# Second block's attention: where eight gate products stand beside the transposed probabilities and the values

## The reference

```python
q, k, v, x_lru, g_lru, gate_attn, gate_lru = split(u @ w_in)
attn = softmax(causal(rope(q) @ rope(k).T * dh ** -0.5)) @ v     # 8 heads of 128, one block of 256 keys
y_attn = attn @ w_branch_attn
xc = causal_depthwise_conv(x_lru)
r, i = sigmoid(block_diag(xc, w_a)), sigmoid(block_diag(xc, w_i))
a = exp(-8 * r * softplus(-lam)); bx = sqrt(1 - a * a) * (i * xc)
h[t] = a[t] * h[t - 1] + bx[t]
y_lru = (h * gelu(g_lru)) @ w_branch_lru
merged = sigmoid(gate_attn) * y_attn + sigmoid(gate_lru) * y_lru
```

## Time and profile before

| what | value |
|---|---|
| median of 3 runs | 1237.03 us (1235.73 to 1237.9) |
| profiled execution, its own time | 1240.2 us |
| its span, first to last instruction | 1238.4 us |
| TensorE busy | 1074.8 us, 87% |
| VectorE, GpSimd, ScalarE busy | 795.8, 735.4, 466.7 us |
| mean granted TensorE clock | 0.982 |

### The profile page before, as it was taken

How to read it: one execution, slowest core, us unless ns; L and a number is a source line. 1 busy time by engine, 2 the same in 40 slices (tenths; PEclk the granted TensorE clock), 3 DMA queues, 4 the chain that set the end, 5 groups by cost and what they waited for, 6 DMA issues and landing times.

```text
span 1238.4 us, 14907 instructions
## 1 busy us (share of the span) xinstructions
PE 1074.8 (87%) x5042; PEld 735.7 (59%) x5042; DVE 795.8 (64%) x1547; ACT 466.7 (38%) x1013; POOL 735.4 (59%) x445
## 2 busy tenths in 40 slices
PE   6898988999877877787777778899999999999998
PEld 5776544454422322232333223899988997988996
DVE  3367988869668577686675556405354553977977
ACT  5664332231221211211212114545666436434443
POOL 6543766666434444254344332786697985978885
PEclk9999999999999999899999999999999999999999
DMA  7627999999999999999999997763454554555552
GB/s 232 248 85 306 357 420 420 420 419 422 420 422 421 422 421 401 401 405 420 423 421 422 419 420 318 255 186 122 137 166 140 188 172 151 187 173 190 184 190 97
DMA packets 66099, 372.27 MB, mean 301 GB/s; under 512 B 7625, under 2 KB 8753, under 8 KB 32945
## 3 DMA queue, kind: packets, MB, share of 16 engines
q0 software_dynamic: 36864, 268.45, 52.5%
q1 hardware_dynamic: 27696, 98.07, 23.9%
q10 hardware_dynamic: 1472, 4.88, 1.2%
HBM read 369.79 MB, written 1.06 MB: 299 GB/s over the span
## 4 chain that ended last, share of the span: by engine, by line
PE 41%; DMA 30%; DVE 15%; ACT 6%; issue 5%; POOL 3%; DVEq 0%; SPq 0%; POOLq 0%; ACTq 0%
DMA arena<-in_peer_uv,idx_all 28%; PE ps L1796 10%; PE ps L1493 9%; PE ps L1494 9%; PE ps L1495 9%; DVE arena L1275 5%; POOL w_hl L423 2%; DVE yT L1463 2%; DVE arena L1461 2%; DMA ring<-in_weights 2%; PE ps L1842 1%; ACT prob L699 1%; DVE wts L1284 1%; POOL arena L433 1%; ACT w_hl L511 1%
## 5 line engine op out<-in xcount | busy, mean ns | idle before, releaser
L1796 PE MATMUL ps<-arena,prob 128*128 128x512 f32 x1024 | 482.4, 618 | 123.1 <-ACT prob L699 122.2
L433 POOL DMA_INDIRECT arena<-in_peer_uv,idx_all x256 | 288.3, 1126 | 357.9 <-PE ps L1796 324.9
L423 POOL TENSOR_TENSOR w_hl<-ring,w_hl 128x1024 fp32r<-128x1024 f32 x161 | 405.2, 2527 | 119.9 <-ACT w_hl L511 118.4
L1796 PEld LDWEIGHTS ps<-arena,prob 128*128 128x128 f32 x1024 | 189.6, 194 | 404.5 <-ACT prob L699 207.2
L1275 DVE CUSTOM_DVE_ANT_0 arena<-arena,xn 128x1024 f32<-128x1024 f32 x256 | 322.5, 1261 | 154.2 <-DMA arena<-in_peer_uv,idx_all 151.5
L1493 PE MATMUL ps<-xT,w_hl 128*128 128x256 f32 x760 | 218.8, 288 | 5.7 <-DVE arena L1353 2.9
L1494 PE MATMUL ps<-xT,w_hl 128*128 128x256 f32 x760 | 216.0, 284 | 0.0
L1495 PE MATMUL ps<-xT,w_hl 128*128 128x256 f32 x760 | 215.9, 284 | 0.0
L511 ACT ACTIVATE w_hl<-ring 128x1024 fp32r<-128x1024 f32 x161 | 169.3, 1057 | 100.5 <-PE ps L1495 92.6
L692 ACT ACTIVATE gel<-acts 128x2 f32<-128x2 f32 (+1 forms) x130 | 26.4, 203 | 401.6 <-DVE acts L1275 401.6
L1493 PEld LDWEIGHTS ps<-xT,w_hl 128*128 128x128 f32 x760 | 146.9, 193 | 7.8 <-issue 4.5
(11 more groups left out here) (301 smaller groups left out, 1214.7 us busy)
## 6 DMA issues: line engine op xcount, KB each, us to landing
ring<-in_weights SPq DMA_DIRECT2D x178, 512.0 KB, 3.5
arena<-in_peer_uv,idx_all POOLq DMA_INDIRECT x256, 13.5
arena<-in_rg_weights ACTq DMA_DIRECT2D x1, 2048.0 KB, 8.2
x<-in_x SPq DMA_DIRECT2D x2, 512.0 KB, 5.1
bias<-rel_scratch SPq DMA_DIRECT2D x1, 1024.0 KB, 7.9
arena<-in_subkeys SPq DMA_DIRECT2D x1, 1024.0 KB, 5.8
out_x<-x ACTq DMA_DIRECT2D x4, 256.0 KB, 2.1
arena<-in_band SPq DMA_DIRECT2D x1, 768.0 KB, 9.4
```

The lines of the kernel that those rows point to most:

```text
L423: pool.tensor_tensor(pair[:, 1], raw(n), pair[:, 0].bitcast(F32), ALU.subtract).then_inc(w_lo, 1)
L433: pool.indirect_dma_start(uv_slot(n), None, A["peer_uv"], bass.IndirectOffsetOnAxis(idx_all[:, h, c:c + 1], 0))\
L1796: j = pe.matmul(banks(2 + 2 * t + half), diag[:, n % GRING, :], uv_slot(n)[:, D + half * 512:D + (half + 1) * 512], start=False, stop=(h = ...
```

## The change

TensorE issues gate products 8, 9 and 10 each behind two of the six groups of transposes, so the values come after product 10; five gate products are left behind the values. ScalarE's order follows: two copies, one gate evacuation with its high half of a weight, three times, then the square root, the four copies to yT and the last five gate evacuations. Nothing else is changed; no instruction is added or left out.

```diff
-            def gate_evacs(first):
-                for m in range(first, first + 8):
+            def gate_evacs(ms):
+                for m in ms:
                     split_hi(W_GATES + m + AHEAD)
                     act.wait_ge(w_used, W_GATES + m + 1)
                     evac_proj(F_GATES + m, projT[:, 32 + m, :], ACT.Sigmoid).then_inc(proj_evac, 1)
 
-            gate_evacs(0)
-            evac_probT(1)
+            gate_evacs(range(8))
+            for turn in range(3):
+                evac_probT(1, range(2 * turn, 2 * turn + 2))
+                gate_evacs(range(8 + turn, 9 + turn))
             act.wait_ge(lru_step, 2)
             act.activation(Rg[:].rearrange("p a b -> p (a b)"), Rg[:].rearrange("p a b -> p (a b)"),
                            ACT.Sqrt).then_inc(sqrt_done, 1)
...
-            gate_evacs(8)
+            gate_evacs(range(11, 16))
...
-            prob_transposes(1)
+            for turn in range(3):
+                prob_transposes(1, range(2 * turn, 2 * turn + 2))
+                product(F_GATES + 8 + turn, W_GATES + 8 + turn, xTc, evacuated(F_GATES + 8 + turn))
             pe.wait_ge(pT_evac, 12)
...
-            for m in range(8, 16):
+            for m in range(11, 16):
                 product(F_GATES + m, W_GATES + m, xTc, evacuated(F_GATES + m))
             pe.wait_ge(aT_lo, 8)
```

## The result

The changed kernel takes 1245.95 us, the median of 6 runs (1243.75 to 1248.89), beside 1236.49 us for the kernel before in 6. The ratio is 1.0076, with a 95% interval of 1.006 to 1.0091: slower by 7 to 11 us. The profiled execution took 1246.51 us over a span of 1244.7. Two executions of the whole series stood far outside, one of the kernel before (1611.45 us) and one of an experiment's kernel (2224.71 us), and are left out of the ratios.

A forecast was written before the change was run, and what follows sets the result against it. TensorE was taken to set the pace, with 2.7 us of slack in the root-to-yT chain. Removed waits -1.9, new wait +8.8, clock +1.5 gave +8.4 us on the 1237.03 median: 1245.4 us, range 1240.8 to 1249.

The forecast's parts named there:

- The waits removed: TensorE at the transposes and values: waits vanish, values start at 950.7, five products end at 970.5 instead of 972.39; 1.9 us gained.
- Weights: Weight halves for the moved gate products: product 10's is ready, high halves come before the root; costed at nothing.
- The square root: ScalarE: the root stands behind the third gate evacuation, so it starts at 952.6 instead of 945.16, 7.4 us later.
- The scans: VectorE's eight scans from 956.9: about three at 0.58 us, five waiting a GpSimd turn of 2.79, ending at 972.6.
- more turns: Rival: GpSimd gets in after two scans, +2.2 us, or the clock stays low twice as long, +1.5; 1247 to 1249, chance 0.15.
- a shared rate: Other reading of VectorE's scans beside GpSimd: they keep their mean of 1.7 us, chain ends at 977.1 instead of 979.3.
- The new wait: TensorE before the first attention-branch product: ready at 970.5, waits for yT's low halves until 979.3, 8.8 us idle.
- The clock: TensorE behind the new idle: some 16 matmuls at 1.2 GHz lose 1.5 us, bounds zero and 3.0.
- the plain shift: Rival: VectorE's chain moves by 7.4 us with no turn lost, net +4.7; 1241.7 to 1243.2 us, chance 0.2.
- The faster one: Rival: VectorE's chain escapes GpSimd, up to two turns of 2.2 us hidden, only 1.9 gained; 1235.1 us, chance 0.05.

The follow-up runs named there:

- the shortened piece: Changed kernel, with GpSimd making only the first 128 of 1024 columns of gate product 14's low weight half: 1236.32 us, ratio 0.9988.

## Why the prediction was right, point by point

The forecast was 1245.4 us, measured 1245.95; the sum was +8.4 us, the stage +8.06.

- **The waits removed.** Forecast 1.9 us. The values start 11.22 us after the first transposes (937.58 to 948.80), as 3 x (0.90 + 2.88) = 11.34 had said, and all three waits are gone. The kernel with the root in product 6 shows the gain by itself, 1.9 and 2.0 us on the stage in two executions; the other two with an early root gain 1.3 and 1.0, as each has a wait of 0.52 us back.
- **Weights.** TensorE has no wait for GpSimd after 930; nothing, as costed.
- **The square root.** Forecast 7.4 us later. Counted from the first transposes, it was 945.16 - 939.35 = 5.81 and is 950.70 - 937.58 = 13.12: 7.3 later. Both directions were run: the root moved up alone takes the loss away, the root moved back alone makes one.
- **The scans.** Forecast one turn more, three quick and five slow, 15.7 us in all; measured 15.60, with three quick and five slow. That the count came out is in part luck. GpSimd came 1.05 us after the first scan, not 1.2, and let only two scans pass before it, which is the condition of the rival "more turns". The third quick scan came only at 964.50. A turn took 2.76 us (scans at 956.23 and 958.99), and GpSimd's pieces started every 2.88 (958.75, 961.63, 964.50), so its pauses grew until one scan got in without a wait. The forecast had said that at this pace the turns follow each other, with no such gap. Had that scan waited too, the chain would have ended 2.2 us later, by an estimate from the rows of 2.83 and 0.66. That it is turns and not a shared rate was the least certain step, and the shortened piece settles it: 8.4 us of scans for 1.84 us of GpSimd's work. The Trainium skill (SBUF — State Buffer, "Who interferes with whom") says that the port pair which the two engines share is an exclusive lock, and the trace agrees: 2.83 us for a scan behind a piece, 0.66 for one alone.
- **The new wait.** Forecast 8.8 us, measured 8.65.
- **The clock.** Forecast 1.5 us, for 16 matmuls at the lower clock, with bounds of zero and 3.0. It was 2.8 us of low clock behind the idle, 13 matmuls; with the idle filled the stage is 1.23 us shorter. That the size came so near is luck: it was taken from the stretch behind an idle of 2.92 us, and two other kernels lost 2.6 us, one behind a longer and one behind a shorter idle. The bounds held in all three. See the last section.

Of the rivals, the plain shift (+4.7) fell with the 15.60 us of scans. The faster one named its condition rightly: it priced a turn at 2.2 us and allowed up to two. In the run with the shortened piece VectorE's chain lost two, one in the scans and one in the multiplication (4.32 us against 2.29), with the root as late as in the change; the idle was 0.29 us and the stage 64.02 us, 1.5 under the kernel before. In the change itself the condition did not hold, since GpSimd was fed right after the first scans.

That the total comes within 0.55 us is in part the baseline's doing. The medians differ by 9.5 us, where 8.4 were forecast and the stage has 8.06; the forecast set its sum on 1237.03 us, and the kernel before came out at 1236.49 over six runs. The 1.4 us between the medians' difference and the stage's are not placed; only the part before the stage was seen to vary by so much.

## What to carry to other kernels

When work is moved ahead on one engine, look at what is queued behind it on the engine that serves it: here the gain of 1.9 us on TensorE was real, and a square root standing behind the moved evacuations cost 10 us of the stage (73.62 against 63.6). Before the move, work out the slack of every chain that starts behind it (2.7 us here), and whether the shift brings that chain against an engine it takes turns with. A long function that depends on nothing near should stand in the serving engine's idle time: the same three products between the transposes then gain their 1.9 us on the stage.

## What the runs showed of the hardware that was not expected

How much of the low clock is left behind an idle spell does not follow the spell's length: 2.8 us behind 8.65, 5.9 us behind 11.66, and 5.9 us behind 2.96. The clock falls inside the spell, and not at the same point of it. In the changed kernel, idle from 968.7, it was 1.00 to 972, 0.73 over the next 3 us and 0.50 from 975 on, so part of the low stretch lay inside the idle, where it costs nothing. With two products between it was still 0.86 over the whole of the short idle. With the late root in the kernel before it had fallen well inside the idle too (0.56 over 972 to 976), and 5.9 us were left all the same. What decides the length is not shown here. The three kernels in this order:

```profile
972.00:975.00 3.00, 0.00 (x0) 0.00 (x0) 3.00 (x2) 0.05 (x1) 0.77 (x1) 0.73 0.52 205
```

```profile
968.30:971.30 3.00, 0.09 (x1) 0.00 (x0) 3.00 (x5) 1.64 (x3) 3.00 (x2) 0.86 0.40 156
```

```profile
972.00:976.00 4.00, 0.00 (x0) 0.00 (x0) 3.96 (x3) 0.00 (x0) 2.80 (x2) 0.56 0.48 157
```

With 7.93 us of an idle of about 8.8 filled, and 0.89 left, there was no low stretch. At 5.9 us it costs about 28 matmuls of 0.21 instead of 0.12 us, 2.6 us, nearly as much as the idle of 2.96 itself.

A matmul of the filler, plain float32 on both sides, took 0.43 us for 256 columns and two records (36 records for 18 in 7.93 us), against 0.12 us and one record for the products' matmuls.
